# A hybrid decoder layer with a mixture of experts: two DRAM accumulators for even and odd expert blocks, and a gather with a limit on the row number

## The chip, the cores and the metric

The kernel runs on one core of one Trainium2 chip. The metric is the device time of one execution in microseconds; less is better. All times and rows below come from one profiled execution of the kernel before, and from its three timed runs.

## What is computed

One decoder layer on 1024 tokens of width 1024, all in float32. First token mixing (three recurrent branches, gates, an output projection and a LayerNorm; the first 1350 us or so of the kernel, of which the change touches only the last part), then a mixture of experts on the result:

```python
def _moe(x2d, ...):                       # x2d: 1024 x 1024
    scores = sigmoid(x2d @ router_w)      # 64 experts, 8 chosen for a token, weights w
    ...                                   # sort the token-expert pairs by expert
    padded = (counts + 127) // 128 * 128  # every expert's rows are padded to blocks of 128
    row_tok = full((n_rows,), N).at[dest].set(tok_flat[order])   # padding slots name row N
    row_w = zeros((n_rows,)).at[dest].set(w_flat[order])         # with weight 0
    def block_fn(acc, inp):
        rows, wts, e = inp
        xb = x_pad[rows]
        yb = _swiglu(xb, w1[e], w3[e], w2[e]) * wts[:, None]
        return acc.at[rows].add(yb), None
    ...
    return routed[:N] + _swiglu(x2d, sw1, sw3, sw2)              # plus one shared expert

x = layernorm(DN_ALPHA * x + ffn, ln2_g, ln2_b)
```

The hidden width of an expert is 256. There are 8,192 token-expert pairs.

## The kernel before

**The data.** `x1_rows` in DRAM holds the 1024 rows after the first LayerNorm and 128 rows of zeros behind them (rows 1024 to 1151, called trash rows here). `ffn_rows` in DRAM has the same shape and is the accumulator: its first 1024 rows start as alpha times x, its trash rows as zeros. The slot table gives each slot of each block of 128 a row number and a weight. Slots that no token fills name a trash row, with weight 0. The shared expert is expert 0 with 8 blocks (0 to 7); the 64 others have one or two blocks each. With these inputs there are 108 blocks. A padding slot is gathered, computed and added like any other: zeros are read from a trash row and zeros are added to a trash row.

**One step of the block loop.** The loop runs over blocks in pairs (`u` is 0 for even and 1 for odd blocks, `b = i * 2 + u`), and is pipelined over five engines that each run their own program in order and meet at semaphores. In step b

- TensorE (`tail_pe`, L605 to L652) transposes `hm` of block b (L639), makes the hidden products of block b+1 (L611 from `xgT`), transposes the gathered rows of block b+2 (L605) and makes the output products of block b (L611 from `hTs`). Each product is made of three with split float32 operands, so each weight and activation has a high and a low part.
- ScalarE (`tail_act`, L676 to L722) copies `hTs` (L711), splits off the high parts of w1/w3 if block b+2 is the first of its expert (`split13`, L681, two instructions) and of w2 if block b+1 is (`split2`, L686), computes silu for block b+1 (L700), copies `xgT` of block b+2 (`rowsT`, L693), and last, once the output products of block b are there and the weight column `wx` is ready (`e_wx`), scales the first half of the output (L722).
- VectorE (`block_step`, L896 to L923) first waits until the scatter of block b-2 has landed (`e_sc`), copies the row numbers `sx` and the weights `wx` of block b (L901, L902), then makes the low part of `hTs` (L905), the first low half of w1/w3 (L870), `hm` of block b+1 (L865), the low part of `xgT` of block b+2 (L883), names the rows of the gather for block b+4 (L894), makes the other low parts (L870), and scales the second half of the output (L923).
- GpSimd (`tail_pool`) issues the gather of block b+4 (L512), waits until the scatter of block b-1 has landed and both halves of the output of block b are ready, and issues the scatter of block b (L529): an indirect DMA that adds 128 rows of 4 KB to `ffn_rows`.
- SyncE loads the weights of an expert, 3 MB, into one of three slots (L396) as soon as the slot is free.

`yo`, `sx` and `wx` have two buffers each, by `u`. Two scatters that add to the same row must not be in flight together, so all scatters stand in one row: each waits for the last.

**Around the loop.** Before it, GpSimd zeroes `sig` (L488) and stores it to the trash rows (L491); SyncE loads the weights of the first experts and a tile of x for each of the eight row tiles (L401), and stores each tile of x1 and of alpha times x1; VectorE needs the x tile for L762, and ScalarE writes alpha times x1 into `sig` (L663) once the zeros have been stored. After the loop SyncE loads `ffn_rows` into `fr` in eight tiles (L470), and VectorE, ScalarE and GpSimd normalise them (L947 to L958, L727, L731, L555).

## Time and profile before

| | us |
|---|---|
| median of 3 runs | 2719.61 (2713.7 to 2730.28) |
| profiled execution | 2750.55 |
| its span | 2747.8 |
| TensorE busy in it | 2375.9 (86%) |
| VectorE busy | 1306.7 (48%) |
| ScalarE busy | 844.0 (31%) |
| GpSimd busy | 598.9 (22%) |

The page of the profile has the busy time of each engine, the chain of work that ended last, and the costliest groups of instructions by line. PE is TensorE, DVE VectorE, ACT ScalarE, POOL GpSimd, SP SyncE. A wait is put down to what released it; "issue" is time in which an engine waited for nothing that the profile shows (branches and register loads among it). Times in the rows are microseconds from the start of the span. The DMA share is the busy share of the core's 16 DMA engines.

### The profile page before, as it was taken

What the parts mean: (1) busy time and instruction counts of PE and PEld (TensorE: products, weight loads), DVE (VectorE), ACT (ScalarE), POOL (GpSimd) and SP (SyncE); (2) the same over time, 40 slices, a digit from 0 to 9 for tenths busy, and PEclk for the clock granted to TensorE, in tenths of its full rate; (3) what the DMA queues carried; (4) which work ended last, traced back from release to release, by engine and by line L of the source; (5) the groups of instructions that cost most, each with busy time, mean ns of one, the idle gap of its engine ahead of it and who ended that gap; (6) DMA issues with size and microseconds to landing.
All of it is one profiled execution on the core that took longest, in us unless ns stands there. A gap on an engine that the chain in (4) does not pass through costs nothing.

```text
span 2747.8 us, 36372 instructions
## 1 busy us (share of the span) xinstructions
PE 2375.9 (86%) x8956; PEld 1541.4 (56%) x8957; DVE 1306.7 (48%) x2144; ACT 844.0 (31%) x1049; POOL 598.9 (22%) x403
## 2 busy tenths in 40 slices
PE   9976878999989999999635888989989989889992
PEld 3454554555545444445323667777767777677771
DVE  6275712243334111114461466665676766565665
ACT  1032111111111110001111456454555645455442
POOL 1000001120202000000036433333333333333333
PEclk9997969999999999999866999999999999999996
DMA  3001001100000111143212589797898988778864
GB/s 143 31 31 24 9 0 69 35 27 31 0 23 23 34 42 38 34 187 133 96 62 46 156 274 313 239 312 229 283 311 239 328 265 257 247 239 277 276 163 160
DMA packets 85449, 390.65 MB, mean 142 GB/s; under 512 B 15361, under 2 KB 15617, under 8 KB 59394
## 3 DMA queue, kind: packets, MB, share of 16 engines
q1 hardware_dynamic: 51522, 274.21, 26.3%
q0 software_dynamic: 33888, 115.95, 17.7%
q8 instruction: 21, 0.34, 0.0%
q14 instruction: 18, 0.15, 0.0%
HBM read 318.47 MB, written 70.47 MB: 142 GB/s over the span
## 4 chain that ended last, share of the span: by engine, by line
PE 39%; DMA 18%; issue 8%; DVE 3%; DVEq 2%; ACT 2%; another core or an unknown queue 1%; POOL 0%; ACTq 0%; POOLq 0%; SPq 0%
DMA ffn_rows<-yo,sx 17%; PE ps L611 14%; PE ps L1265 10%; PE ps L1273 5%; PE ps L566 4%; PE ps L1127 2%; DVEq L375 1%; PE ps L605 1%; PE ps L1301 1%; DVE yo L923 1%; ACT xgT L693 1%; PE ps L639 1%; PE ps L584 1%; ACT wts L681 1%
## 5 line engine op out<-in xcount | busy, mean ns | idle before, releaser
L611 PE MATMUL ps<-wts,xgT 128*128 x2616 | 652.8, 405 | 28.0 <-issue 22.9
L611 PEld LDWEIGHTS ps<-wts,xgT 128*128 128x128 f32 x2616 | 494.3, 192 | 163.0 <-issue 52.5
L870 DVE TENSOR_TENSOR wts<-wts (+1 forms) x195 | 443.9, 2289 | 120.5 <-issue 88.6
L611 PE MATMUL ps<-wts,hTs 128*128 x1296 | 362.8, 431 | 82.9 <-DVE hTs L905 58.5
L611 PEld LDWEIGHTS ps<-wts,hTs 128*128 128x128 f32 x1296 | 256.4, 205 | 151.5 <-issue 97.8
L1265 PE MATMUL ps<-xT,ring 128*128 128x512 f32 x768 | 334.7, 593 | 0.0
L1127 PE MATMUL ps<-xT,ring 128*128 128x512 f32 x704 | 311.4, 599 | 6.1 <-DMA ring<-in_w_in 6.1
L529 POOL DMA_INDIRECT ffn_rows<-yo,sx x108 | 216.9, 2009 | 387.8 <-DVE yo L923 191.9
L512 POOL DMA_INDIRECT xg<-x_rows,ix x112 | 200.5, 1790 | 378.5 <-DVE ix L894 366.0
L681 ACT ACTIVATE wts<-wts (+1 forms) x130 | 241.8, 1908 | 75.2 <-issue 75.2
L1265 PEld LDWEIGHTS ps<-xT,ring 128*128 128x128 f32 x768 | 145.2, 190 | 178.9 <-issue 178.9
L1127 PEld LDWEIGHTS ps<-xT,ring 128*128 128x128 f32 x704 | 133.2, 192 | 164.1 <-issue 164.1
L883 DVE TENSOR_TENSOR xgT<-ps,xgT 128x512 fp32r<-128x512 f32 x220 | 141.6, 685 | 76.3 <-ACT xgT L693 74.6
L722 ACT ACTIVATE yo<-ps,wx 128x512 f32<-128x512 f32 x108 | 74.3, 688 | 299.4 <-PE ps L611 274.8
L605 PE MATMUL ps<-ident,xg 128*128 128x128 f32 x880 | 117.9, 276 | 50.4 <-DMA xg<-x_rows,ix 36.9
L1372 ACT ACTIVATE sig<-ps,chan 128x512 f32<-128x512 f32 x48 | 33.0, 687 | 386.4 <-PE ps L1265 349.4
L1798 DVE TENSOR_TENSOR sig<-sig,ps 128x512 f32<-128x512 f32 x32 | 22.0, 688 | 271.8 <-PE ps L1273 271.8
L605 PEld LDWEIGHTS ps<-ident,xg 128*128 128x128 f32 x880 | 104.4, 142 | 66.4 <-DMA xg<-x_rows,ix 37.4
L686 ACT ACTIVATE wts<-wts (+1 forms) x65 | 124.0, 1908 | 51.8 <-issue 51.8
L693 ACT ACTIVATE xgT<-ps 128x512 fp32r<-128x512 f32 x220 | 119.2, 594 | 63.2 <-PE ps L605 61.2
L865 DVE TENSOR_TENSOR hm<-si,ps 128x256 f32<-128x256 f32 x109 | 45.8, 420 | 165.2 <-ACT si L700 143.0
L1074 POOL MEMSET Gd<- 128x1024 f32 x4 | 4.0, 1012 | 539.1 <-DVE u_tok L1783 420.2
(359 smaller groups left out, 2290.1 us busy)
## 6 DMA issues: line engine op xcount, KB each, us to landing
wts<-in_experts SPq DMA_DIRECT2D x195, 1024.0 KB
ring<-in_w_in SPq DMA_DIRECT2D x52, 512.0 KB, 3.3
bring<-in_w_branch SPq DMA_DIRECT2D x24, 256.0 KB, 2.6
xT<-in_xT SPq DMA_DIRECT2D x4, 1024.0 KB, 9.2
wout<-in_w_out SPq DMA_DIRECT2D x1, 4096.0 KB, 12.4
N<-in_x SPq DMA_DIRECT2D x8, 512.0 KB, 3.3
x_rows<-N SPq DMA_DIRECT2D x8, 512.0 KB, 2.6
ffn_rows<-sig SPq DMA_DIRECT2D x8, 512.0 KB, 2.8
```

The source lines that it names most:

```text
L512: g.indirect_dma_start(out=xg[:, k, :], out_offset=None, in_=x1d, in_offset=bass.IndirectOffsetOnAxis(ap=ix[:, k:k + 1], axis=0)).then_inc ...
L529: g.indirect_dma_start(out=accd, out_offset=bass.IndirectOffsetOnAxis(ap=sx[:, u:u + 1], axis=0), in_=yo[:, u, :], in_offset=None, compute ...
L605: ins = tr(ps[q // 4][:, (q % 4) * P:(q % 4 + 1) * P], xg[:, k, q * P:(q + 1) * P], ident[:])
L611: ins = mm(o, left(x), slot_cols(s, w, slice(c0, c0 + HALF)), start=first and n == 0, stop=last and n == 2)
L681: A(slot_cols(s, 1, cols), slot_cols(s, 0, cols).bitcast(F32), ACT.Copy).then_inc(e_hih, 1)
L686: A(slot_cols(s, 1, W2), slot_cols(s, 0, W2).bitcast(F32), ACT.Copy).then_inc(e_hio, 1)
L693: ins = A(xgT[:, k, 1, 4 * b:4 * b + 4, :].rearrange("p a b -> p (a b)"), ps[b][:], ACT.Copy)
L870: tt(w, w.bitcast(F32), hi, ALU.subtract).then_inc(done, 1)
L883: ins = tt(v(0), ps[b][:], v(1).bitcast(F32), ALU.subtract)
L1127: ins = mm(ps[b][:], ring[:, slot, k, :], xT[:, k, h * HALF:(h + 1) * HALF], start=k == 0, stop=k == KD - 1)
L1265: ins = mm(ps[h][:], ring[:, 4 + s, k, :], xT[:, k, h * HALF:(h + 1) * HALF], start=k == 0, stop=k == KD - 1)
L1273: ins = mm(ps[2 + h][:], bring[:, s, k, :], y[:, k, h * HALF:(h + 1) * HALF], start=k == 0, stop=k == WT - 1)
```

## The change

The accumulator becomes two tables in DRAM, `ffn_rows0` for even blocks and `ffn_rows1` for odd ones, each with its own semaphore. The second starts as zeros: GpSimd stores `sig` nine times, 128 rows each. A scatter now waits only for the last one of its own table, two blocks back. At the end both tables are loaded, into `fr` and `fs`, and VectorE adds them tile by tile before the LayerNorm. The gather gets a limit: rows with a number above 1023 are skipped, and their places in `xg` keep what lay in them; their weight is 0. On VectorE the wait for the scatter and the copies of `sx` and `wx` stand no longer at the start of the step but behind the low parts of the weights, just ahead of the wait for the output products. ScalarE's own waits in the loop stay as they are.

```diff
--- before.py
+++ after.py
@@
 NBT = NBMAX + 4
 TRASH = P
 NROW = T + TRASH
+SC0 = (16 * 2, 16 * (KD + 1))
 ALPHA = 2.0 ** 0.25
 LN_EPS, RMS_EPS = 1e-5, 1e-6
 BIG = 1e30
@@ -118,7 +119,7 @@
 
 
         x1d = nc.dram_tensor("x1_rows", [NROW, D], F32, kind="Internal").ap()
-        accd = nc.dram_tensor("ffn_rows", [NROW, D], F32, kind="Internal").ap()
+        accd = [nc.dram_tensor(f"ffn_rows{i}", [NROW, D], F32, kind="Internal").ap() for i in range(2)]
         slotd = nc.dram_tensor("slot_table", [P * NBT, 2], I32, kind="Internal").ap()
         blockd = nc.dram_tensor("block_table", [2 * P, 4], I32, kind="Internal").ap()
 
@@ -205,6 +206,7 @@
 
         lay_f = ExitStack()
         fr = sbx(lay_f, "fr", [P, KD, D])
+        fs = sbx(lay_f, "fs", [P, KD, D])
         lay_f.close()
         lay_m = ExitStack()
 
@@ -268,6 +270,7 @@
         a_go = sem("act_waited")
         p_go = sem("pool_waited")
         d_go = sem("dve_waited")
+        sp_go = sem("sp_waited")
         w_full = [sem(f"w_full{i}") for i in range(6)]
         b_full = [sem(f"bw_full{i}") for i in range(2)]
         k_full = [sem(f"bank_full{i}") for i in range(4)]
@@ -353,7 +356,7 @@
         e_wx = sem("row_weight_ready")
         e_ya = sem("output_half_act")
         e_yd = sem("output_half_dve")
-        e_sc = sem("rows_adding")
+        e_sc = [sem(f"rows_adding{i}") for i in range(2)]
         e_ix = sem("gather_rows_named")
         f_in = [sem(f"ffn_rows_loaded{i}") for i in range(KD)]
         f_var = sem("ffn_variance")
@@ -465,9 +468,12 @@
             announce(w_o, 63 % 3, (63 // 3 + 1) * 16, s_wo2)
             announce(w_o, 64 % 3, (64 // 3 + 1) * 16, s_wo2)
             n = counts(sp)
-            sp.wait_ge(e_sc, n * 32 + 32)
+            for k in range(2):
+                sp.wait_ge(e_sc[k], n * 16 + SC0[k])
+                sp.sem_inc(sp_go, 1)
             for t in range(KD):
-                sp.dma_start(fr[:, t], accd[t * P:(t + 1) * P, :]).then_inc(f_in[t], 16)
+                for rows, part in zip((fr, fs), accd):
+                    sp.dma_start(rows[:, t], part[t * P:(t + 1) * P, :]).then_inc(f_in[t], 16)
             for t in range(KD):
                 store_out(sp, t)
             sp.wait_ge(f_out, 16 * KD)
@@ -476,7 +482,7 @@
             sp.wait_ge(s_x1, t + 1)
             sp.dma_start(x1d[t * P:(t + 1) * P, :], x1[:, t % 2]).then_inc(s_x1s[t % 2], 16)
             sp.wait_ge(s_xa, t + 1)
-            sp.dma_start(accd[t * P:(t + 1) * P, :], sig[:, :, :].rearrange("p a b -> p (a b)")).then_inc(s_xas, 16)
+            sp.dma_start(accd[0][t * P:(t + 1) * P, :], sig[:, :, :].rearrange("p a b -> p (a b)")).then_inc(s_xas, 16)
 
         def store_out(sp, t):
             sp.wait_ge(f_y, t + 1)
@@ -488,7 +494,9 @@
             g.memset(sig[:], 0.0).then_inc(s_z, 1)
             pool.wait_ge(s_z, 1)
             for r in (slice(0, TRASH // 2), slice(TRASH // 2, TRASH)):
-                pool.dma_start(accd[T:NROW][r], sig[r, :, :].rearrange("p a b -> p (a b)")).then_inc(e_sc, 16)
+                pool.dma_start(accd[0][T:NROW][r], sig[r, :, :].rearrange("p a b -> p (a b)")).then_inc(e_sc[0], 16)
+            for t in range(KD + 1):
+                pool.dma_start(accd[1][t * P:(t + 1) * P, :], sig[:, :, :].rearrange("p a b -> p (a b)")).then_inc(e_sc[1], 16)
 
             pool.wait_ge(s_lg, KD)
             g.iota(slt[:, 0:SHB, 0:1], pattern=[[P, SHB], [0, 1]], base=0, channel_multiplier=1).then_inc(s_slt0, 1)
@@ -504,13 +512,15 @@
             for k in range(2):
                 pool.wait_ge(s_x1s[k], 8 * KD)
             pool.wait_ge(s_zd, 16)
-            pool.wait_ge(e_sc, 32)
+            for k in range(2):
+                pool.wait_ge(e_sc[k], SC0[k])
             pool.wait_ge(s_xas, 16 * KD)
 
             def gather(k):
 
                 g.indirect_dma_start(out=xg[:, k, :], out_offset=None, in_=x1d,
-                                     in_offset=bass.IndirectOffsetOnAxis(ap=ix[:, k:k + 1], axis=0)).then_inc(e_g[k], 16)
+                                     in_offset=bass.IndirectOffsetOnAxis(ap=ix[:, k:k + 1], axis=0),
+                                     bounds_check=T - 1, oob_is_err=False).then_inc(e_g[k], 16)
 
             def named_gather(c):
 
@@ -520,14 +530,15 @@
                 ch.link(g.tensor_copy(ix[:, c % 2:c % 2 + 1], slt[:, c, 0:1]))
                 gather(c % 2)
 
-            def add_rows(b, u):
-
-                pool.wait_ge(e_sc, b * 16 + 32)
+            def add_rows(i, u):
+
+                b = i * 2 + u
+                pool.wait_ge(e_sc[u], i * 16 + SC0[u])
                 pool.wait_ge(e_ya, b + (1 + ONE))
                 pool.wait_ge(e_yd, b + (1 + ONE))
                 pool.sem_inc(p_go, 1)
-                g.indirect_dma_start(out=accd, out_offset=bass.IndirectOffsetOnAxis(ap=sx[:, u:u + 1], axis=0),
-                                     in_=yo[:, u, :], in_offset=None, compute_op=ALU.add).then_inc(e_sc, 16)
+                g.indirect_dma_start(out=accd[u], out_offset=bass.IndirectOffsetOnAxis(ap=sx[:, u:u + 1], axis=0),
+                                     in_=yo[:, u, :], in_offset=None, compute_op=ALU.add).then_inc(e_sc[u], 16)
 
             for c in range(4):
                 named_gather(c)
@@ -539,16 +550,15 @@
                 if b + 4 == SHB:
                     pool.wait_ge(s_slt, 16)
                 named_gather(b + 4)
-                add_rows(b, b % 2)
+                add_rows(b // 2, b % 2)
             n = counts(pool)
             with pool.Fori(SHB // 2, n) as i:
                 for u in range(2):
-                    b = i * 2 + u
                     pool.wait_ge(e_ix, i * 2 + (u + 1 - SHB))
                     pool.wait_ge(e_T, i * 2 + (u + 3))
                     pool.sem_inc(p_go, 1)
                     gather(u)
-                    add_rows(b, u)
+                    add_rows(i, u)
 
             for t in range(KD):
                 pool.wait_ge(f_g, t + 1)
@@ -657,7 +667,8 @@
                 if t >= 1:
                     act.wait_ge(s_x1, t)
                     act.wait_ge(s_zd, 16)
-                    act.wait_ge(e_sc, 32)
+                    for k in range(2):
+                        act.wait_ge(e_sc[k], SC0[k])
                     if t >= 2:
                         act.wait_ge(s_xas, 16 * (t - 1))
                     A(sig[:, :, :].rearrange("p a b -> p (a b)"), x1[:, (t - 1) % 2], ACT.Copy, scale=ALPHA).then_inc(s_xa, 1)
@@ -896,10 +907,6 @@
             def block_step(i, u, named):
 
                 b = i * 2 + u
-                dve.wait_ge(e_sc, i * 32 + (16 * u + 16))
-                dve.sem_inc(d_go, 1)
-                V.tensor_copy(sx[:, u:u + 1], slt[:, bass.ds(b, 1), 0:1].rearrange("p o w -> p (o w)")).then_inc(e_wx, 1)
-                V.tensor_copy(wx[:, u:u + 1], sltf[:, bass.ds(b, 1), 1:2].rearrange("p o w -> p (o w)")).then_inc(e_wx, 1)
                 dve.wait_ge(e_hTe, i * 2 + (u + 1) + ONE)
                 h_ = lambda x: hTs[:, x].rearrange("p a b -> p (a b)")
                 tt(h_(0), ps[4][:, 0:2 * P], h_(1).bitcast(F32), ALU.subtract).then_inc(e_hTl, 1)
@@ -918,6 +925,10 @@
                 o, s, first = block_entry(dve, i * 2 + (u + 1))
                 with dve.If(first > 0):
                     split2(o, s)
+                dve.wait_ge(e_sc[u], i * 16 + SC0[u])
+                dve.sem_inc(d_go, 1)
+                V.tensor_copy(sx[:, u:u + 1], slt[:, bass.ds(b, 1), 0:1].rearrange("p o w -> p (o w)")).then_inc(e_wx, 1)
+                V.tensor_copy(wx[:, u:u + 1], sltf[:, bass.ds(b, 1), 1:2].rearrange("p o w -> p (o w)")).then_inc(e_wx, 1)
                 dve.wait_ge(e_Y, i * 2 + (u + 1) + ONE)
                 dve.wait_ge(e_wx, i * 4 + (2 * u + 2))
                 ts(yo[:, u, HALF:D], ps[7][:], wx[:, u:u + 1], None, ALU.mult).then_inc(e_yd, 1)
@@ -940,9 +951,10 @@
 
             for t in range(KD + 2):
                 if t < KD:
-                    dve.wait_ge(f_in[t], 16)
+                    dve.wait_ge(f_in[t], 32)
                     if t >= 2:
                         dve.wait_ge(f_n, t - 1)
+                    L(tt(fr[:, t], fr[:, t], fs[:, t], ALU.add))
                     for h in range(2):
                         N(V.bn_stats(fst[:, t % 2, h], fr[:, t, h * HALF:(h + 1) * HALF]))
                     ch.wait()
```

## Rows read from the trace of the kernel before

**Rows 1.** The page, part 4: the chain that ended last, by line.

```profile
DMA ffn_rows<-yo,sx 17%; PE ps L611 14%; PE ps L1265 10%; PE ps L1273 5%; PE ps L566 4%; PE ps L1127 2%; DVEq L375 1%; PE ps L605 1%; PE ps L1301 1%; DVE yo L923 1%; ACT xgT L693 1%; PE ps L639 1%; PE ps L584 1%; ACT wts L681 1%
```

**Rows 2.** Stages: length, busy time (instructions) by engine; then granted clock, DMA share, GB/s.

```profile
1570.49:2685.14 1114.65, 1008.11 (x4555) 793.65 (x4556) 715.71 (x981) 587.07 (x682) 385.39 (x197) 0.97 0.83 266
1975.00:2035.00 60.00, 50.90 (x226) 39.27 (x225) 47.98 (x55) 36.37 (x39) 21.13 (x10) 0.97 1.01 354
...
1216.00:1242.00 26.00, 24.28 (x63) 11.19 (x63) 7.68 (x11) 2.44 (x4) 2.28 (x3) 1.00 0.87 339
```

**Rows 3.** Timeline, TensorE: start, us, line, what, idle before.

```profile
2675.09 0.41 PE L639 MATMUL ps<-ident,hm 128*128 128x128 f32 x2 [0.37 <-issue]
...
2685.14 0.38 PE L639 MATMUL ps<-ident,hm 128*128 128x128 f32 x2
```

**Rows 4.** Waits, 1570 to 2685: waiting line, releaser, us in total, times, longest.

```profile
ACT yo L722 <- PE ps L611: 264.4, 99, 7.7
...
POOL ffn_rows L529 <- DMA ffn_rows<-yo,sx: 165.9, 33, 7.0
DVE sx L901 <- DMA ffn_rows<-yo,sx: 130.5, 35, 6.6
ACT si L700 <- PE ps L611: 115.2, 74, 5.7
```

**Rows 5.** The chain that ended last, in order of time: start, us, what.

```profile
2012.33 11.40 DMA ffn_rows<-yo,sx
...
2024.62 11.74 DMA ffn_rows<-yo,sx
...
2697.28 5.82 DMA ffn_rows<-yo,sx
```

**Rows 6.** Timeline, ScalarE.

```profile
2064.76 0.69 ACT L722 ACTIVATE yo<-ps,wx 128x512 f32<-128x512 f32 x1 [6.12 <-PE ps L611]
...
2066.12 3.72 ACT L681 ACTIVATE wts<-wts  x2 [0.40 <-issue]
...
2074.23 0.69 ACT L722 ACTIVATE yo<-ps,wx 128x512 f32<-128x512 f32 x1 [1.78 <-PE ps L611]
...
2076.12 3.72 ACT L681 ACTIVATE wts<-wts  x2 [0.83 <-issue]
...
2081.83 1.08 ACT L693 ACTIVATE xgT<-ps 128x512 fp32r<-128x512 f32 x2
...
2086.90 1.92 ACT L686 ACTIVATE wts<-wts  x1 [1.21 <-issue]
```

**Rows 7.** Timeline, VectorE.

```profile
2063.96 2.29 DVE L870 TENSOR_TENSOR wts<-wts  x1 [2.06 <-issue]
...
2072.49 1.29 DVE L883 TENSOR_TENSOR xgT<-ps,xgT 128x512 fp32r<-128x512 f32 x2 [1.16 <-ACT xgT L693]
...
2074.03 2.29 DVE L870 TENSOR_TENSOR wts<-wts  x1 [0.19 <-issue]
...
2084.51 4.50 DVE L870 TENSOR_TENSOR wts<-wts  x2 [0.21 <-issue]
...
2089.64 0.14 DVE L902 COPY wx<-slt 128x1 f32 x1
```

**Rows 8.** Groups by line, 1570.4 to 2685: count, busy us, mean ns, idle before.

```profile
L681 ACT ACTIVATE wts<-wts x124 | 230.7, 1909 | 40.5 <-issue 40.5
...
L686 ACT ACTIVATE wts<-wts x63 | 120.3, 1909 | 51.8 <-issue 51.8
```

**Rows 9.** Timeline, VectorE, ahead of the router.

```profile
1242.72 0.69 DVE L762 SCALAR_TENSOR_TENSOR N<-N,ps 128x512 f32<-128x512 f32 x1 [4.45 <-DMA N<-in_x]
1246.60 0.69 DVE L762 SCALAR_TENSOR_TENSOR N<-N,ps 128x512 f32<-128x512 f32 x1 [3.19 <-PE ps L566]
```

**Rows 10.** Timeline, VectorE, behind the loop.

```profile
2716.17 1.21 DVE L958 TENSOR_TENSOR fr<-fr,ln 128x1024 f32<-128x1024 f32 x1
...
2719.74 1.21 DVE L958 TENSOR_TENSOR fr<-fr,ln 128x1024 f32<-128x1024 f32 x1
```

## Prediction, written before the change was run

> **What bounds the kernel now.** I read the page first: 17% of the chain that ended last is one transfer, `ffn_rows<-yo,sx`, the adding scatter of an expert block [rows 1]. So part of the time is not TensorE's. The stages place it [rows 2]: the block loop has 108 blocks, and from the hm transpose of block 8 (1570.49) to that of block 107 (2685.14) it takes 1114.65 us for 99 steps, 11.26 us each. A step that nothing holds up takes 10.05 us, as the last two transposes show [rows 3]: its products stand back to back. At that pace the 99 steps would take 995 us; 120 us are stalls.
>
> The list of waits says whose [rows 4]: VectorE waited 130.5 us in 35 cases before L901 (`sx`) for a scatter to land, GpSimd 165.9 us in 33 cases to issue the next one. The chain shows the loop that this makes [rows 5]: issued, 11.4 us until landed, under a microsecond, issued again; one step each 12.3 us. Beside weight loads a scatter needs 11 to 12 us, the last one of all, with nothing beside it, 5.82. Block b+1 may add only when block b has landed, and VectorE starts step b only when b-2 has. Those two waits are what the change attacks.
>
> **What the change removes.** Each table takes every second block, so scatter b waits for b-2 and not for b-1. That one was issued two steps (20 us) before and takes 12 [rows 5]. Both waits of [rows 4] go, and even a scatter that takes half as long again beside a second one is in time. If nothing else were touched, the gain would lie between 0 and the 120 us of stalls.
>
> **What the change moves, and this decides.** The two small copies `sx` and `wx` (L901, L902) go from the start of VectorE's step to behind `split13(.., 1)` and `split2`. `wx` isn't for VectorE alone: ScalarE waits for it (`e_wx`) before its half of the output, L722, and ScalarE works in order. Behind L722 are queued the next step's hTs copy (L711), both splits (L681, L686), silu (L700) and rowsT (L693). VectorE's hm and its low part of xgT (L883) need silu and rowsT, and TensorE's next products need L883. Today L722 waits for TensorE alone, 264.4 us in 99 cases [rows 4], and starts ahead of VectorE's last split: at 2074.23, where that ends at 2076.32 [rows 6, 7]. After the change a ring runs through both engines: L722, L711, L681, L686, L700, L693, then on VectorE L883, L894, L870, `sx`, `wx`, then L722 of the next step. The two engines work side by side now; then they take turns.
>
> The length of the ring depends on the step. Call it A where ScalarE splits w1/w3 of a coming expert (two L681), B where it splits w2 (L686), AB where it does both. From 1570.4 to 2685 there are 124 L681, so 62 steps with them, and 63 L686 [rows 8], in 99 steps. One step, the last, has neither, so 62 + 63 + 1 - 99 = 27 are AB, 35 are A and 36 are B. The lengths, from [rows 6] for ScalarE and [rows 7] for VectorE:
>
> - *AB.* From L722 (2074.23) to the end of L693 (2082.91) 8.68, back to back but for a gap of 0.83 ahead of L681. VectorE: from L883 (2072.49) to the end of one L870 (2076.32) 3.83, and with two (4.50 in place of 2.29) 6.04. `sx`, `wx` and the hand-overs between the engines: 0.34, an estimate from 0.14 for the `wx` copy. Sum 15.1. Ahead of L681 the gap is also seen as 0.40: 14.65. I take 14.9.
> - *A.* From L722 (2064.76) to the end of L681 (2069.84) 5.08, with the short gap. L686, silu and rowsT took 3.07 (2079.84 to 2082.91); without L686 (1.9, 0.1 of it overlapped) 1.27. VectorE 3.83, and 0.34. Sum 10.5, with the longer gap 10.9: 10.7.
> - *B.* L722 and L711 take 0.96 (2064.76 to 2065.72), a gap of 1.21 where the branch around `split13` is jumped, L686 1.92, then 1.27: 5.36. VectorE has one L870, but ahead of it a gap of 2.06 and not 0.19: 5.70. And 0.34. Sum 11.4; with the difference of 0.4 between gaps 11.8: 11.6.
>
> All three are above TensorE's 10.05, so the ring sets every step: 27 x 14.9 + 35 x 10.7 + 36 x 11.6 + 10.05 = 1204.5 us against 1114.65: **+90** (all gaps short 1184, +69; all long 1224, +109). TensorE's work of a step runs beside it. Blocks 0 to 7 I leave at 0: they have no splits.
>
> **The gather's limit.** Padding slots name rows from 1024 up. The 100 expert blocks have 12,800 slots, 8,192 of them real (1,024 tokens, 8 experts each): 4,608 rows of 4 KB are not moved. The gather is given two steps, and no wait of TensorE for it stands among the large ones [rows 4], so it is worth nothing on the path. It would pay where the DMA engines are the bound, from 1975 to 2035 with a share of 1.01 [rows 2]; steps of 14.9 us take that pressure away as well. If the limit costs GpSimd time, that is hidden too: it is busy 385 of 1114 us [rows 2].
>
> **The zeroing of the second table.** Nine more stores of 512 KB by GpSimd, right where six weight loads run: DMA share 0.87 from 1216 to 1242 [rows 2]. 4.7 MB more at the 354 GB/s of the full stretch are 13 us; they push back the second x tile, for which VectorE waits until 1242.72. Of that, 3.2 are covered by its wait for TensorE just behind (1246.60) [rows 9]. **+7**, between 0, if the stores slip in beside the loads, and 10. ScalarE's first write of `sig` waits for the same stores, beside this wait.
>
> **The end.** Sixteen loads in place of eight, and one addition of 128x1024 per tile. VectorE paces the tiles, 3.57 us each (2716.17 to 2719.74), and an operation of this size is L958, 1.21 [rows 10]; with 0.1 for its link, 8 x 1.31 = 10.5. The second load of the first tile adds about 1. **+11.5**, between 9 and 15. The two loads of a tile, 1 MB at 354 GB/s, take 3 us, less than the 4.9 of the work.
>
> **Sum.** 90 + 7 + 11.5 = +108.5 us. The profiled execution has a span of 2747.8 and took 2750.55, 31 more than the median of 2719.61. The sum is made against its span, and I add the difference to the median: **2828 us**; with all low terms 2798, with all high ones 2854. A difference of 1% is about what can be told from none.
>
> **The rivals.**
> *Faster: the ring doesn't bind.* If ScalarE had enough slack behind L722, the stalls would simply go. For it: ScalarE idles ahead of silu for 115.2 us [rows 4], 1.2 a step, and that much lateness is free. Against it: L722 moves by 2 us behind an A step and by over 4 behind AB and B; this decides below 1.2. The DMA engines would then bind where single-block experts follow each other: steps of 12.3 us at a share of 1.01 [rows 2, 5]. With 12 for the 27 AB steps, 27 x 12 + 72 x 10.05 = 1048 us, -67, and +18.5 for the fixed parts: 2671. The Trainium skill ("DMA: Bandwidth & Descriptors", Issuing engines are not separate DMA queues) says that all DMAs interleave on the same 16 engines whoever issues them; by that a second table adds no bandwidth, and the AB steps could not come down to 10.05 (which would give 2618). By that rule, the share of 1.01 agrees. Chance 12%.
> *About the same: part of the ring overlaps.* If the gap of 2.06 in the B step were hidden once VectorE waits elsewhere, that step falls to 9.5, under TensorE's 10.05. With short gaps in the others 27 x 14.65 + 35 x 10.5 + 37 x 10.05 = 1135 us, +20, and 18.5: 2758. Against it: the gap stands behind a copy of 0.14 us, at the end of the step, where VectorE has nothing to wait for. Chance 10%, half of it within 1%.
> *Slower still: TensorE's clock.* It is granted 0.97 over the loop and over the stretch from 1975 [rows 2]. The AB steps would leave TensorE idle for 5 us each. If products at the lower level outlast the ring, steps grow; at 1 us for each AB step +27: to 2880. Chance 10%.
>
> **Chances.** The ring as summed 68%, of its own 2798 to 2854; the clock 10%, part of the ring 10%, no ring 12%. Faster by over 1%: 0.12, within 1%: 0.05, slower by over 1%: 0.83. The range goes down to the partial ring and up to the clock: 2750 to 2880.
>
> **What would show it.** Right: ScalarE's idle time ahead of L722 is put down to DVE `wx` and no longer to TensorE; the waits of VectorE and GpSimd for `ffn_rows` are near 0; steps of 15 us where both splits are; VectorE idle ahead of L865 and L883, for ScalarE; a lower DMA share in the loop; in the software queue at least 4,608 packets less for the gathers and 1,152 more for the zeroing. Wrong: steps of 10 to 12 us throughout and L722 released by TensorE. The number is off most if the gaps around jumped branches shrink or grow.

## The result, and the profile after

The changed kernel takes 2818.32 us (median of four runs, 2809.79 to 2821.0), the kernel before 2719.93 beside it: a ratio of 1.0344, with a 95% interval of 1.0317 to 1.037. It is slower, by 98 us. Of the profiled execution the span is 2816.7 us.

The stages, each from its first instruction to that of the next, in us; "router" runs from the first product of the output projection to the last router scores, the loop is that of [rows 2]. The second run of the changed kernel, on another chip, stands beside the first:

| | before | after | after, again |
|---|---|---|---|
| up to the output projection | 1217.9 | 1222.0 | 1224.1 |
| router | 140.8 | 155.8 | 155.7 |
| to the hm transpose of block 0 | 71.0 | 70.5 | 70.5 |
| blocks 0 to 7 | 140.8 | 119.1 | 139.5 |
| loop, 99 steps from block 8 | 1114.6 | 1165.5 | 1163.5 |
| end, from block 107 | 62.7 | 83.7 | 83.6 |
| span | 2747.8 | 2816.7 | 2836.9 |

So the loop costs 49 to 51 us more, the router stage 15, the end 21. Blocks 0 to 7 were 22 us shorter in this one profile; in the twelve others of this study, the second run of the same kernel among them, they took 138 to 141. That belongs to the execution, not to the change. The execution profiled before had been 31 us above its median, this one is 1 above its own; that is why 69 us of span answer to 98 us between the medians.

The page of the kernel after: two parts of the chain that ended last (by engine, by line), then the group of ScalarE's half of the output.

```profile
PE 37%; issue 12%; ACT 7%; DVE 7%; DVEq 4%; ACTq 3%; POOL 3%; DMA 2%; POOLq 0%; SPq 0%
PE ps L621 14%; PE ps L1277 10%; PE ps L1285 5%; PE ps L576 3%; DVE wts L881 3%; ACT wts L692 2%; POOL slot_table L548 2%; ACT xgT L704 2%; DVEq L378 2%; PE ps L1139 2%; ACTq L378 2%; ACT wts L697 2%; PE ps L615 2%; DMA ffn_rows<-sig 1%; PE ps L1313 1%
...
L733 ACT ACTIVATE yo<-ps,wx 128x512 f32<-128x512 f32 x108 | 74.4, 689 | 529.0 <-DVE wx L931 522.6
```

The scatter, 17% of the chain before [rows 1], is gone from it. In its place stand ScalarE, VectorE and their queues: the splits L692, L697 and L881 (L681, L686 and L870 before), and the copy of xgT, L704 (L693). The waits of the loop in the kernel after, which answer to [rows 4] (us in total, times, longest):

```profile
ACT yo L733 <- DVE wx L931: 501.7, 99, 6.3
POOL ffn_rows L540 <- DVE yo L934: 235.7, 95, 8.0
DVE hm L876 <- ACT si L711: 154.1, 65, 4.5
DVE wts L881 <- ACT wts L692: 146.1, 62, 2.8
...
ACT si L711 <- PE ps L621: 5.4, 5, 2.4
```

ScalarE waited for TensorE before its half of the output, 264.4 us; now it waits for VectorE's copy `wx`, in each of the 99 steps, 501.7 us. No engine waits for a scatter any more. ScalarE's slack ahead of silu, 115.2 us before, is down to 5.4. The ring can be followed in ScalarE's timeline of the kernel after, through a step AB, a step B and a step A (start, us, line, what, idle before and its releaser):

```profile
2048.57 0.69 ACT L733 ACTIVATE yo<-ps,wx 128x512 f32<-128x512 f32 x1 [6.27 <-DVE wx L931]
...
2049.84 3.72 ACT L692 ACTIVATE wts<-wts  x2 [0.32 <-issue]
2053.47 1.90 ACT L697 ACTIVATE wts<-wts  x1
...
2055.53 1.07 ACT L704 ACTIVATE xgT<-ps 128x512 fp32r<-128x512 f32 x2
2062.84 0.69 ACT L733 ACTIVATE yo<-ps,wx 128x512 f32<-128x512 f32 x1 [6.24 <-DVE wx L931]
...
2065.36 1.91 ACT L697 ACTIVATE wts<-wts  x1 [1.55 <-issue]
...
2067.88 1.09 ACT L704 ACTIVATE xgT<-ps 128x512 fp32r<-128x512 f32 x2 [0.33 <-PE ps L615]
2074.11 0.69 ACT L733 ACTIVATE yo<-ps,wx 128x512 f32<-128x512 f32 x1 [5.15 <-DVE wx L931]
...
2084.40 0.69 ACT L733 ACTIVATE yo<-ps,wx 128x512 f32<-128x512 f32 x1 [4.05 <-DVE wx L931]
```

and in VectorE's, over the same stretch:

```profile
2056.63 1.29 DVE L894 TENSOR_TENSOR xgT<-ps,xgT 128x512 fp32r<-128x512 f32 x2 [0.55 <-ACT xgT L704]
...
2058.19 4.50 DVE L881 TENSOR_TENSOR wts<-wts  x2 [0.21 <-issue]
...
2062.66 0.15 DVE L931 COPY wx<-slt 128x1 f32 x1
...
2068.99 1.29 DVE L894 TENSOR_TENSOR xgT<-ps,xgT 128x512 fp32r<-128x512 f32 x2 [0.90 <-ACT xgT L704]
...
2071.66 2.29 DVE L881 TENSOR_TENSOR wts<-wts  x1 [1.31 <-issue]
```

In the first of these steps ScalarE works 8.03 us, from L733 to the end of L704 (2056.60). VectorE does what it can of the step meanwhile and then waits for L704; it begins L894 0.03 later and works until `wx` is written, 2062.81. ScalarE stands still for those 6.24 us and begins L733 0.03 later. So the two stretches add up, and the step is 14.27 long. The spacing of L733 over the loop, by kind, is 14.45 for AB, 10.46 for A and 11.00 for B.

### The profile page after: what moved, and what is told of

It reads as the page before. It is cut to its first block, busy times and chain, and to the rows that moved or that the text cites. A ratio compares the mean times of both kernels' runs of the same rounds, so it can differ in the third digit from the quotient of the medians.

```text
span 2816.7 us, 36513 instructions
## 1 busy us (share of the span) xinstructions
PE 2392.1 (85%) x8956; PEld 1554.7 (55%) x8957; DVE 1341.2 (48%) x2152; ACT 826.8 (29%) x1049; POOL 564.1 (20%) x412
## 3 DMA queue, kind: packets, MB, share of 16 engines
q0 software_dynamic: 35184, 99.72, 16.4%
## 4 chain that ended last, share of the span: by engine, by line
PE 37%; issue 12%; ACT 7%; DVE 7%; DVEq 4%; ACTq 3%; POOL 3%; DMA 2%; POOLq 0%; SPq 0%
PE ps L621 14%; PE ps L1277 10%; PE ps L1285 5%; PE ps L576 3%; DVE wts L881 3%; ACT wts L692 2%; POOL slot_table L548 2%; ACT xgT L704 2%; DVEq L378 2%; PE ps L1139 2%; ACTq L378 2%; ACT wts L697 2%; PE ps L615 2%; DMA ffn_rows<-sig 1%; PE ps L1313 1%
## 5 line engine op out<-in xcount | busy, mean ns | idle before, releaser
L621 PE MATMUL ps<-wts,xgT 128*128 x2616 | 689.9, 423 | 109.7 <-issue 107.7
L621 PEld LDWEIGHTS ps<-wts,xgT 128*128 128x128 f32 x2616 | 522.6, 203 | 255.1 <-issue 134.4
L881 DVE TENSOR_TENSOR wts<-wts (+1 forms) x195 | 444.3, 2291 | 212.1 <-ACT wts L692 150.7
L621 PE MATMUL ps<-wts,hTs 128*128 x1296 | 332.1, 405 | 0.0
L521 POOL DMA_INDIRECT xg<-x_rows,ix x112 | 207.3, 1851 | 593.4 <-DVE ix L905 575.3
L621 PEld LDWEIGHTS ps<-wts,hTs 128*128 128x128 f32 x1296 | 238.3, 191 | 49.8
L692 ACT ACTIVATE wts<-wts (+1 forms) x130 | 241.8, 1907 | 64.0 <-DMA btab<-block_table 33.0
L733 ACT ACTIVATE yo<-ps,wx 128x512 f32<-128x512 f32 x108 | 74.4, 689 | 529.0 <-DVE wx L931 522.6
L540 POOL DMA_INDIRECT ffn_rows<-yo,sx x108 | 170.2, 1576 | 255.4 <-DVE yo L934 246.4
L894 DVE TENSOR_TENSOR xgT<-ps,xgT 128x512 fp32r<-128x512 f32 x220 | 141.8, 686 | 97.4 <-ACT xgT L704 95.4
L704 ACT ACTIVATE xgT<-ps 128x512 fp32r<-128x512 f32 x220 | 118.8, 594 | 72.2 <-PE ps L615 72.1
L697 ACT ACTIVATE wts<-wts (+1 forms) x65 | 124.0, 1908 | 48.4 <-issue 48.4
L576 PE MATMUL ps<-wout,mixT 128*128 128x512 f32 x256 | 114.3, 601 | 1.7 <-issue 1.7
## 6 DMA issues: line engine op xcount, KB each, us to landing
ffn_rows<-sig POOLq DMA_DIRECT2D x9, 512.0 KB, 24.3
```

Source lines behind the costliest of these rows:

```text
L521: g.indirect_dma_start(out=xg[:, k, :], out_offset=None, in_=x1d, in_offset=bass.IndirectOffsetOnAxis(ap=ix[:, k:k + 1], axis=0), bounds_c ...
L540: g.indirect_dma_start(out=accd[u], out_offset=bass.IndirectOffsetOnAxis(ap=sx[:, u:u + 1], axis=0), in_=yo[:, u, :], in_offset=None, comp ...
L576: ins = mm(ps[b][:], mixT[:, k, t * P:(t + 1) * P], wout[:, k, h * HALF:(h + 1) * HALF], start=k == 0, stop=k == KD - 1)
L621: ins = mm(o, left(x), slot_cols(s, w, slice(c0, c0 + HALF)), start=first and n == 0, stop=last and n == 2)
L692: A(slot_cols(s, 1, cols), slot_cols(s, 0, cols).bitcast(F32), ACT.Copy).then_inc(e_hih, 1)
L697: A(slot_cols(s, 1, W2), slot_cols(s, 0, W2).bitcast(F32), ACT.Copy).then_inc(e_hio, 1)
```

## The experiments

All times are medians beside the kernel before on the same chip, where that took 2740 to 2744 us; so they are compared by their ratios. Loop, router and end are stages as in the table above. "AB after AB" is the mean step from one hm transpose to the next where two blocks in a row split both sets of weights (12 steps, the second of each such pair): 11.56 before, 14.43 after.

| kernel | us | ratio (95%) | router | loop | end | AB after AB |
|---|---|---|---|---|---|---|
| after_again | 2835.53 | 1.0351 (1.0328, 1.0375) | 155.7 | 1163.5 | 83.6 | 14.48 |
| a_wx_early | 2676.77 | 0.9753 (0.9723, 0.9784) | 155.8 | 1005.9 | 83.8 | 10.34 |
| b_move_alone | 2797.92 | 1.0195 (1.017, 1.022) | 140.8 | 1160.6 | 63.4 | 14.35 |
| c_tables_no_move | 2770.69 | 1.0095 (1.0067, 1.0123) | 155.6 | 1097.1 | 83.2 | 11.79 |
| d_no_limit | 2831.66 | 1.0322 (1.0298, 1.0347) | 155.7 | 1161.3 | 83.3 | 14.49 |
| e_one_table_wx_early | 2656.65 | 0.9678 (0.9661, 0.9696) | 140.8 | 1019.4 | 63.2 | 11.38 |
| f_one_table_wx_early_limit | 2650.43 | 0.9647 (0.9629, 0.9666) | 140.8 | 1015.3 | 63.0 | 11.30 |
| g_ends | 2651.97 | 0.9655 (0.9629, 0.968) | 140.8 | 1007.9 | 71.8 | 10.34 |
| h_copies_earlier | 2669.83 | 0.9734 (0.9706, 0.9762) | 155.5 | 1000.4 | 83.8 | 10.23 |
| i_one_table_earlier | 2647.99 | 0.966 (0.9638, 0.9682) | 140.8 | 1013.8 | 63.8 | 11.32 |
| j_two_tables_best | 2644.55 | 0.9654 (0.9629, 0.9678) | 140.8 | 1000.6 | 71.8 | 10.24 |

**after_again: the changed kernel as it is.**

> The changed kernel once more, beside the others. Blocks 0 to 8 took 119 us in its profile and 138 to 141 in every other kernel's, also in those that differ from it in one edit behind block 7. If that is the kernel's own, it is 119 again; if it belongs to the run or the chip, it is about 140, and its ratio to before nears the sum of the stages, 15 + 51 + 21 = 87 us or 1.032.

Ratio 1.0351 beside 1.0344: the same on another chip. Blocks 0 to 7 took 139.5 us this time, so the 119 was not the kernel's own; but the ratio did not come nearer to 1.032, the sum of the stages, as was expected with it.

**a: is it the copy `wx`?** The kernel after, with `wx` copied at the start of the step and `sx` left late, under a semaphore of its own. ScalarE now waits for the scatter b-2 itself, since it overwrites `yo` (the last part of the diff):

```diff
+                V.tensor_copy(wx[:, u:u + 1], ...).then_inc(e_wx, 1)
                 dve.wait_ge(e_hTe, i * 2 + (u + 1) + ONE)
...
-                V.tensor_copy(sx[:, u:u + 1], ...).then_inc(e_wx, 1)
-                V.tensor_copy(wx[:, u:u + 1], ...).then_inc(e_wx, 1)
+                V.tensor_copy(sx[:, u:u + 1], ...).then_inc(e_sx, 1)
...
+                    act.wait_ge(e_sc[u], i * 16 + SC0[u])
+                    act.sem_inc(a_go, 1)
                     act.wait_ge(e_Y, i * 2 + (u + 1) + ONE)
```

> The changed kernel with one thing taken back: the copy of wx stands at the start of VectorE's step again, and only sx, which the scatter needs, stays late; ScalarE and VectorE each wait for the scatter of block b-2 before they write yo. Theory (a ring through ScalarE and VectorE over wx makes the changed kernel slow): the ring is cut, L722's successor is released by TensorE again, the 99 steps take 1010 to 1060 us and not 1165, so the kernel takes some 2700 us, faster than before. Rival (two scatters in flight, or the second table, make it slow): it stays at 2800 to 2820.

The loop falls from 1165.5 to 1005.9 us, just under the 1010 to 1060 expected and near the 995 that TensorE alone would need, and the whole to 0.9753 of before. From the list of waits of its loop (L736 is L733 here):

```profile
ACT yo L736 <- PE ps L622: 167.4, 99, 1.7
ACT si L712 <- PE ps L622: 111.4, 73, 5.7
```

ScalarE waits for TensorE again, and its slack ahead of silu is back. One copy of 0.14 us and its place were worth 160 us. The longest of the 99 steps takes 11.89 us, and AB after AB takes 10.34, against 11.38 with one table and the same order (e, below); so two tables do lift what the scatters set.

**b: the move alone, in the kernel before.** One table, no limit; the wait and both copies are moved to where the change puts them.

```diff
-                dve.wait_ge(e_sc, i * 32 + (16 * u + 16))
-                dve.sem_inc(d_go, 1)
-                V.tensor_copy(sx[:, u:u + 1], ...)
-                V.tensor_copy(wx[:, u:u + 1], ...)
                 dve.wait_ge(e_hTe, i * 2 + (u + 1) + ONE)
...
                     split2(o, s)
+                dve.wait_ge(e_sc, i * 32 + (16 * u + 16))
+                dve.sem_inc(d_go, 1)
+                V.tensor_copy(sx[:, u:u + 1], ...)
+                V.tensor_copy(wx[:, u:u + 1], ...)
```

> The kernel before with the move alone: the wait for the scatter and the copies of sx and wx stand behind the low parts of the weights; one table, no limit, no zeroing, no second load. Theory (ring): the steps are as long as in the changed kernel, 14.5 us for AB, 10.5 for A and 11 for B, 1160 to 1180 us for the 99, while the beginning and the end are those of before; 2780 us, or 50 to 60 over before. Rival (the move is harmless and the two tables cost the time): 2720 as before, or less.

Loop 1160.6, ends as before. The loop of the change is all in this one edit: with steps of 14.35 us the scatters' order in one table no longer matters either. VectorE does not wait for a scatter once in this loop, with one table; GpSimd still does, 64.4 us ahead of the gather and 4.3 ahead of the scatter, off the path.

**c: everything but the move.** The kernel after, with the wait and both copies back at the start of VectorE's step.

```diff
                 b = i * 2 + u
+                dve.wait_ge(e_sc[u], i * 16 + SC0[u])
+                dve.sem_inc(d_go, 1)
+                V.tensor_copy(sx[:, u:u + 1], ...)
+                V.tensor_copy(wx[:, u:u + 1], ...)
                 dve.wait_ge(e_hTe, i * 2 + (u + 1) + ONE)
...
                     split2(o, s)
-                dve.wait_ge(e_sc[u], i * 16 + SC0[u])
-                dve.sem_inc(d_go, 1)
-                V.tensor_copy(sx[:, u:u + 1], ...)
-                V.tensor_copy(wx[:, u:u + 1], ...)
```

> The changed kernel without the move: two tables, limit, zeroing and second load, but the wait and both copies at the start of VectorE's step as before. Theory (ring): no ring; VectorE still waits at times for the scatter of b-2, which takes 12 us beside weights, but no scatter waits for the last; the 99 steps take 1050 to 1100 us, and with 36 us more at both ends (as the traces show) the kernel takes 2690 to 2750. Rival (two tables are slow): 2800 or more.

The loop is 17.5 us shorter than before, no more (1097.1, at the upper end of what was expected), and the ends cost 36: 1.0095. The 2770.69 us lie over the expected 2690 to 2750, on a chip where before took 22 us more than beside the first result. Most of the stalls of before stay, as the waits of this kernel's loop show:

```profile
ACT yo L733 <- PE ps L621: 262.6, 99, 6.7
...
DVE sx L912 <- DMA ffn_rows<-yo,sx: 131.1, 28, 6.2
```

GpSimd's wait is gone, VectorE's (130.5 us before [rows 4]) is not. It comes at the start of step b for the scatter b-2, which was issued only one step before; only GpSimd's stands two steps behind. So the second table needs some move of that wait, and the change moved too much along with it.

**d: without the limit on the gather.**

```diff
-                                     in_offset=bass.IndirectOffsetOnAxis(ap=ix[:, k:k + 1], axis=0),
-                                     bounds_check=T - 1, oob_is_err=False).then_inc(e_g[k], 16)
+                                     in_offset=bass.IndirectOffsetOnAxis(ap=ix[:, k:k + 1], axis=0)).then_inc(e_g[k], 16)
```

> The changed kernel without the limit on the gather's row number. Theory: the gather has two steps of time and TensorE never waits for it in the loop, so the time stays within 0.3% of the changed kernel's 2818, with 4,600 to 5,100 packets more in the software queue. Rival (the skipped rows help by relieving the DMA engines, or cost GpSimd time): 10 us or more to either side.

1.0322 beside 1.0344 and 1.0351, loop 1161.3 beside 1163.5 and 1165.5. The limit gains nothing here. The 4,600 to 5,100 packets more in the software queue did not come: it has 35,184 with and without the limit.

**e and f: one table with the order mended, and the limit on it.** e is the kernel before with `wx` alone at the start of the step and the wait, with `sx`, late. f is e with the limit.

```diff
-                dve.wait_ge(e_sc, i * 32 + (16 * u + 16))
-                dve.sem_inc(d_go, 1)
-                V.tensor_copy(sx[:, u:u + 1], ...)
                 V.tensor_copy(wx[:, u:u + 1], ...)
...
                     split2(o, s)
+                dve.wait_ge(e_sc, i * 32 + (16 * u + 16))
+                dve.sem_inc(d_go, 1)
+                V.tensor_copy(sx[:, u:u + 1], ...)
...
                     rowsT(u, i * 2 + (u + 3), i * 2 + (u + 1))
+                    act.wait_ge(e_sc, i * 32 + (16 * u + 16))
+                    act.sem_inc(a_go, 1)
                     act.wait_ge(e_Y, i * 2 + (u + 1) + ONE)
```

> The kernel before with one table, no limit, no zeroing, and the order of the kernel that cut the ring: wx copied at the start of VectorE's step without a wait, sx late, ScalarE and VectorE each waiting for the scatter of block b-2 before they write yo. Scatter b still waits for b-1. Theory: most of the 120 us of stalls came from VectorE standing still at the start of its step, not from the row of scatters itself, which takes 6 to 12.3 us and about 1 more per step; so the 99 steps take 1020 to 1060 us, the slow ones where AB steps follow each other, and with the short beginning and end of the kernel before it takes 60 to 95 us less than before, as little as the two tables or less. Rival (the row of scatters is the limit, and only a second table lifts it): within 30 us of before.

> The same with the limit on the gather's row number. Theory: where the DMA engines are full, in runs of AB steps, and the row of scatters is tight, 4,608 rows less to move shorten gather and scatter; 0 to 15 us less than without the limit. Rival: nothing, as in the changed kernel, because most padding rows are in second blocks, where the DMA engines have time.

e: loop 1019.4, ratio 0.9678: 95 us of the loop come from the order alone, without a second table. Its waits, and its chain in order of time where AB steps follow each other (blocks 43 to 47):

```profile
POOL ffn_rows L530 <- DMA ffn_rows<-yo,sx: 313.9, 53, 8.7
...
ACT yo L725 <- DMA ffn_rows<-yo,sx: 195.1, 58, 5.2
```

```profile
1932.66 10.98 DMA ffn_rows<-yo,sx
...
1945.47 11.32 DMA ffn_rows<-yo,sx
...
1957.59 10.71 DMA ffn_rows<-yo,sx
...
1978.38 10.51 DMA ffn_rows<-yo,sx
```

The row of scatters still sets these steps (11.38), but it no longer holds up VectorE's low parts of the weights: VectorE's waits for a scatter, 130.5 us before, are down to 0.3. f against e: medians 6 us apart, the loop 4, the intervals overlapping. With one table, where the scatters are in the chain, the limit may be worth these few us; it isn't shown.

**h: another place for the copies.** The kernel after; the wait and both copies go up by a few lines, behind the naming of the gather and ahead of the splits.

```diff
                     name_gather(u, i * 2 + (u + 4))
+                dve.wait_ge(e_sc[u], i * 16 + SC0[u])
+                dve.sem_inc(d_go, 1)
+                V.tensor_copy(sx[:, u:u + 1], ...)
+                V.tensor_copy(wx[:, u:u + 1], ...)
                 o, s, first = block_entry(dve, i * 2 + (u + 2))
...
                     split2(o, s)
-                dve.wait_ge(e_sc[u], i * 16 + SC0[u])
-                dve.sem_inc(d_go, 1)
-                V.tensor_copy(sx[:, u:u + 1], ...)
-                V.tensor_copy(wx[:, u:u + 1], ...)
```

> The changed kernel with the wait for the scatter and both copies some lines further up: behind the low part of xgT and the naming of the gather, ahead of the second half of split13 and of split2. Nothing else differs. Theory (ring): the ring loses the low parts, 4.5 us of 14.45 in AB, 2.3 of 10.46 in A, 2.3 and a gap of 1.3 of 11.0 in B, so 10, 8.2 and 7.4 us; TensorE's 10.05 sets the pace and the 99 steps take 1005 to 1040 us. The kernel is 120 to 160 us faster than the changed one and about as fast as the one with wx at the start. Rival (it is ScalarE's wait for VectorE as such, at any place late in the step): 1100 us or more.

Loop 1000.4, the shortest and a little under the 1005 expected: the ring is opened by not having L881 (2.3 to 4.5 us) in it, with no new semaphore. It is not ScalarE's wait for VectorE as such that costs the time.

**g: what the two ends cost.** a, with the second table zeroed from rows of `x_rows` that hold zeros, each store behind the x1 tile of its number, so that `sig` and the early loads are left alone; and the bias addition of the LayerNorm (L565) moved from GpSimd to VectorE.

```diff
+            pool.wait_ge(s_zd, 16)
             for t in range(KD + 1):
-                pool.dma_start(accd[1][t * P:(t + 1) * P, :], sig[...]).then_inc(e_sc[1], 16)
+                if t < KD:
+                    pool.wait_ge(s_x1, t + 1)
+                pool.dma_start(accd[1][t * P:(t + 1) * P, :], x1d[T:NROW, :]).then_inc(e_sc[1], 16)
...
-                g.tensor_tensor(fr[:, t], fr[:, t], ln2[:, 1], ALU.add).then_inc(f_y, 1)
...
-                    for k in range(2):
-                        act.wait_ge(e_sc[k], SC0[k])
+                    act.wait_ge(e_sc[0], SC0[0])
...
-                    tt(x, x, ln2[:, 0], ALU.mult).then_inc(f_g, 1)
+                    L(tt(x, x, ln2[:, 0], ALU.mult))
+                    tt(x, x, ln2[:, 1], ALU.add).then_inc(f_y, 1)
```

> The kernel with two tables that cut the ring, with both ends changed. The second table is zeroed from the zero rows of x1_rows, one tile behind each x1 tile, so ScalarE's first write of sig doesn't wait for it; and the last addition of the LayerNorm is on VectorE and no longer on GpSimd. Theory: the beginning is longer by 15 us because ScalarE waits for the nine stores, and the end by 21 and not 11 because VectorE's addition takes 3.3 us and not 1.2 beside GpSimd's; so the beginning comes back to 141 to 144 us from the output projection to the scores (156 with the stores as they were), each addition of the two tables takes 1.2 us, a tile 5.5 us and not 6.4, and the end is 5 to 10 us shorter than 83. Rival for the beginning (the DMA engines' load delays the x tile, whoever waits): 150 or more. Rival for the end (3.3 us are the addition's own): tiles of 7.5 us.

The router stage is back at 140.8, and the end falls from 83.8 to 71.8 with one more addition on VectorE than before the edit: 12 us, where 5 to 10 were expected. The ratio goes from a's 0.9753 to 0.9655. The rows stand in the next section.

**i and j: the best of each.** i is the kernel before with the limit and the copies placed as in h; j is h with both ends of g.

> The kernel before with the limit and with the wait and both copies behind the naming of the gather; one table, no second semaphore, no extra wait on ScalarE. Theory: the place of the copies is worth nearly the whole gain, the second table little; 99 steps in 1005 to 1025 us, the beginning 141 and the end 63 us, so 3 to 4% under before. Rival (one table makes VectorE wait in the middle of its step for a scatter that is itself held up): 1040 us or more in the loop.

> Two tables, limit, copies behind the naming of the gather, the second table zeroed from x_rows, the last addition on VectorE. Theory: 1000 to 1005 us for the 99 steps, 141 for the beginning and 72 for the end; within 0.3% of the one-table kernel of this call, since the 9 us that a second load and addition cost eat what the second table brings in the loop.

0.966 and 0.9654, the same within their intervals. Two tables make the loop 13 us shorter than one (1000.6 and 1013.8) and the end 8 longer. The change's own idea is worth next to nothing once the order is right. The order is worth 3.4% against before with the limit (i), 3.2% without it (e).

## Why the prediction was right, and where its numbers were off

**The ring: right.** L733 is released by VectorE's `wx` in 99 of 99 steps. Moved alone (b) it brings the whole loss of the loop, taken out (a, h) it brings the whole loss back and the stalls of before as well. Its length was over-estimated: +90 against +51. By kind, 14.9 was 14.45, 10.7 was 10.46 and 11.6 was 11.00, which is 26 x 0.45 + 35 x 0.24 + 36 x 0.60 = 42 us. From the L733 of block 8 to that of block 107 there are 26 AB steps and 2 with neither (8.96 each), where I had 27 and 1, which makes 7 more: 1155.8 us, 49 under my 1204.5. Counted from hm transpose to hm transpose the loop is 1165.5, 39 under it, since the L733 of block 8 starts 20.7 us behind its transpose and that of block 107 only 11.0. Two of the parts that I had put in from elsewhere were off: the copies and hand-overs, set at 0.34, take 0.18 (from the end of L881, 2062.69, to L733 0.15, and 0.03 into L894), and the gaps behind jumped branches came out differently. In the stretch shown the gap ahead of the two splits L692 is 0.32, under both of the values that I had averaged (0.40, 0.83). In B, VectorE's is 1.31 and not 2.06, and ScalarE's 1.55 and not 1.21. So a gap behind a branch, read in another order of the work, was off by 0.3 to 0.8 us here, once or twice in a step; what sets its length no run shows.

**Both waits for scatters go: right, but not by the tables alone.** I wrote that scatter b-2 "was issued two steps (20 us) before". That holds where GpSimd waits. VectorE's old wait stood at the start of its step, one step behind that issue; c, with two tables, shows it alive, 131.1 us, and b, with one table and the move, shows it gone. It went because of the move.

**The gather's limit at nothing: right** (d). What I had written of its packets was wrong. I expected 4,608 fewer in the software queue. The rows of the page, of the kernel after:

```profile
DMA packets 87897, 378.62 MB, mean 134 GB/s; under 512 B 20753, under 2 KB 21009, under 8 KB 61842
...
q0 software_dynamic: 35184, 99.72, 16.4%
```

and of i, which has the limit but no second table:

```profile
DMA packets 85450, 369.72 MB, mean 140 GB/s; under 512 B 20481, under 2 KB 20737, under 8 KB 59394
...
q0 software_dynamic: 33888, 95.00, 16.2%
```

The kernel before has 85,449 packets with 390.65 MB, 15,361 of them under 512 B, and 33,888 in the software queue. With the limit the count stays and 5,120 packets have become small: 20,481 - 15,361. The bytes fall by 20.9 MB, 5,120 rows of 4 KB. A skipped row saves its bytes and not its packet. (5,120 and not 4,608: the four gathers past the last block name padding rows only.) The pair that differs in the limit alone says the same: d has 15,633 packets under 512 B and the kernel after 20,753. The second table adds 1,296 to the software queue and not 1,152: by the counts each of its nine stores has 16 small packets beside its 128 rows.

**The router stage: +7 predicted, +15 measured.** The step that failed is the sentence that ScalarE's write of `sig` waits for the same stores "beside this wait". It is behind it. ScalarE and TensorE in the kernel after:

```profile
1259.87 1.06 ACT L674 ACTIVATE sig<-N 128x1024 f32<-128x1024 f32 x1 [21.07 <-DMA ffn_rows<-sig]
1260.84 1.07 ACT L678 ACTIVATE N<-ps 128x512 f32<-128x512 f32 x2
...
1261.96 3.68 PE L594 MATMUL ps<-rwt,N 128*128 128x64 f32 x16 [11.37 <-ACT N L678]
1265.42 8.80 PE L576 MATMUL ps<-wout,mixT 128*128 128x512 f32 x16
```

TensorE in the kernel before, at the same place of the work:

```profile
1246.33 1.89 PE L584 MATMUL ps<-rwt,N 128*128 128x64 f32 x16
...
1248.06 7.08 PE L566 MATMUL ps<-wout,mixT 128*128 128x512 f32 x16
```

and the stores' row of the page:

```profile
ffn_rows<-sig POOLq DMA_DIRECT2D x9, 512.0 KB, 24.3
```

Nine stores, issued from 1224.6 on beside the weight loads, land after 24.3 us in the median. L674 needs all of them, since it overwrites `sig`. Behind L674 in ScalarE's queue is L678, and the router's products wait for that, 11.37 us. Then they run slower. The granted clock behind that pause, the columns as in [rows 2], is 0.50, the lower of TensorE's two levels (1.2 GHz):

```profile
1262.00:1265.40 3.40, 3.40 (x16) 3.40 (x17) 3.18 (x4) 0.09 (x1) 0.00 (x0) 0.50 0.77 281
```

The 16 router products take 3.68 us in place of 1.89, and the 16 products of the output projection behind them 8.80 in place of 7.08. 11.37 + 1.79 + 1.72 = 14.9 us, the whole +15; I had priced the clock as a rival in the loop and not here. The second x tile was also late, as predicted: VectorE took it up at 1255.47, 33.5 us after the output projection began, and at 24.8 before [rows 9]. In g, with the stores out of the way of both waits (g does not tell them apart; the second x tile is taken up 25.2 us after the projection began):

```profile
1238.70 1.06 ACT L674 ACTIVATE sig<-N 128x1024 f32<-128x1024 f32 x1 [3.60 <-DVE N L761]
```

I had sized the transfer and its first waiter, and not asked what stands behind the second waiter in its queue. That is the same question that decided the loop.

**The end: +11.5 predicted, +21 measured.** VectorE does pace the tiles, but its addition beside GpSimd's is not 1.21. VectorE and GpSimd in the kernel after:

```profile
2764.20 1.23 DVE L957 TENSOR_TENSOR fr<-fr,fs 128x1024 f32<-128x1024 f32 x1 [1.38 <-ACT fr L742]
...
2768.59 3.27 DVE L957 TENSOR_TENSOR fr<-fr,fs 128x1024 f32<-128x1024 f32 x1 [0.24 <-ACT fr L742]
...
2775.02 3.26 DVE L957 TENSOR_TENSOR fr<-fr,fs 128x1024 f32<-128x1024 f32 x1 [0.24 <-ACT fr L742]
```

```profile
2768.43 2.34 POOL L565 TENSOR_TENSOR fr<-fr,ln 128x1024 f32<-128x1024 f32 x1 [21.26 <-DVE fr L970]
```

With nothing on GpSimd the addition takes 1.23. Where L565 has begun just before, it takes 3.27: L565 ends at 2770.77, and the addition 1.09 later. It stands until GpSimd is done. The tiles are 6.43 apart, 2775.02 less 2768.59, and not 4.9; in g, with two additions more on VectorE than in the kernel before and none on GpSimd, 5.32. Eight additions over the end, in the kernel after and in g, where GpSimd does nothing there:

```profile
L957 DVE TENSOR_TENSOR fr<-fr,fs 128x1024 f32<-128x1024 f32 x8 | 20.0, 2496 | 14.9 <-DMA fs<-ffn_rows 12.3 <-ACT fr L742 2.6
```

```profile
L960 DVE TENSOR_TENSOR fr<-fr,fs 128x1024 f32<-128x1024 f32 x8 | 9.8, 1221 | 14.3 <-DMA fs<-ffn_rows 12.9 <-ACT fr L744 1.4
```

The Trainium skill ("SBUF — State Buffer", SBUF: two separate sides) has this: a VectorE operation with two inputs in SBUF and a GpSimd operation that reads SBUF exclude each other for a whole instruction, whichever starts first. The rows agree, and the Trainium skill could have sized this term ahead. So could the trace of before, in small. VectorE at its end, for the second tile, when GpSimd's L555 has not yet begun, and for a later one:

```profile
2712.51 0.16 DVE L954 SCALAR_TENSOR_TENSOR fmv<-fmv 128x1 f32<-128x1 f32 x1
...
2719.22 0.60 DVE L954 SCALAR_TENSOR_TENSOR fmv<-fmv 128x1 f32<-128x1 f32 x1
```

An operation on 128x1 that takes 0.16 alone took 0.60 beside L555: it also stood until GpSimd's had ended. The new addition is the first such operation of a tile now, and takes over that standing. So a tile grows by 2.04 for the standing, less the 0.44 that L966 (L954 before) no longer stands, and by 1.25 for the addition itself: 3.57 + 1.25 + 1.60 = 6.42.

**The sum.** 90 + 7 + 11.5 was forecast, 51 + 15 + 21 = 87 was measured, so that errors of 18 us at the two ends and one of 39 in the loop partly cancel. The sum was 21.5 us too high by the stages and 10 by the medians. That the forecast of 2828 lies so near to 2818 is in part luck: it owes something to this, and something to the 10 us between stages and medians that stay open. Blocks 0 to 7 at nothing is right by all runs but one.

**The rivals.** *The ring doesn't bind* is out for this kernel, and a shows what it would have been: 2676.77 where I had 2671 (on a chip where before took 22 us more). But its working was wrong. I had AB steps of 12 us from the DMA engines, and held that a second table could not bring them down to 10.05; in a and h they take 10.0 to 10.3. The whole loop of a, of e and of the kernel after (length, busy time by engine; granted clock, DMA share, GB/s):

```profile
1584.13:2590.04 1005.91, 970.56 (x4555) 769.65 (x4554) 718.93 (x981) 585.71 (x682) 346.95 (x197) 1.00 0.85 275
```

```profile
1570.86:2590.26 1019.40, 976.84 (x4555) 773.01 (x4554) 721.40 (x981) 578.99 (x682) 357.68 (x197) 0.99 0.89 291
```

```profile
1567.44:2732.93 1165.49, 1028.24 (x4554) 805.02 (x4555) 732.62 (x983) 570.23 (x683) 345.57 (x197) 0.95 0.75 237
```

The DMA engines move more per time in a than in the changed kernel (275 against 237 GB/s), and the loop is 160 us shorter. Nor did a share of 1.01 over 60 us [rows 2] set the steps there. From the hm transpose of block 43 to that of block 48, in the kernel before and in a:

```profile
1968.42:2028.88 60.46, 51.92 (x231) 40.08 (x230) 45.40 (x53) 39.95 (x41) 21.44 (x10) 0.97 1.01 355
```

```profile
1940.45:1992.03 51.58, 48.91 (x231) 38.82 (x230) 45.73 (x55) 39.13 (x40) 20.83 (x10) 1.00 1.03 375
```

The same blocks pass in 51.6 us in place of 60.5, at a share that is no lower. a has the limit and so fewer bytes to move; f, with the limit and one table, takes 56.7. Before, these steps were set by the time that one scatter takes to land before the next may start, and that went with the second table. How far the DMA engines are from binding in a isn't shown. *Part of the ring overlaps* is out: all three kinds are above 10.05. *TensorE's clock*: granted 0.95 over the loop against 0.97 before [rows 2] and 1.00 in a. Products do stretch a little (1028 us busy against 971 in a), but ScalarE waits for them only 5.4 us ahead of silu and 8.2 ahead of L704 in the whole loop, so it costs next to nothing there. Where it did cost time is the router stage, 3.5 us.

**Open:** why blocks 0 to 7 took 119 us in one profile and 138 to 141 in the others. In the longer ones TensorE has gaps between single products of blocks 0 to 4 that no wait explains, in the kernel before 1.1 to 2.9 us each; the short one has none of them over 1 us. And 87 us of stages stand against 96 to 98 between the medians; the profiles are single executions, and the difference of 10 was not tried.

## What to carry to other kernels

When an operand's copy is moved, ask who else reads it, and what is queued behind that reader. Two engines that had worked side by side can be joined in one ring, and then each step is as long as both. Copy small operands that another in-order engine waits for before the long work of the step, and put only what truly depends on a late event behind its wait; here that was worth 160 us, and the second table 13.

Where an operation is added to VectorE, look at what GpSimd does at that moment, not only at the operation's own length. And before buying a structure to break a dependency, try the existing one with its waits in better places: i does with one table all that j does with two, within the intervals.

## What was not expected of the hardware

- A gather row that the limit skips stays as a packet under 512 B: 15,361 such packets became 20,481, and the number of packets in the software queue stayed at 33,888.
- A VectorE addition of 128x1024 takes 1.22 us, and 3.27 when a GpSimd addition of 2.34 us has begun 0.16 before it.
- A DMA share of 1.01 did not mean that the steps could not be shorter: blocks 43 to 47 took 60.5 us at a share of 1.01 before, and 51.6 us at 1.03 in a.
- After a pause of 11.37 us in the router stage TensorE's granted clock was 0.50 for the next 3.4 us, and its 16 products took 3.68 us in place of 1.89.
- The gap behind a jumped branch isn't a constant: VectorE's was 2.06 and 1.31 us, ScalarE's 1.21 and 1.55, for the same code in another order of the work.
